# One fused two-block model on one Trainium2 core: conditioning groups reordered, their rows spread by the tensor engine, a thirteenth expert slot, the root table asked for ahead

## The reference, cut to what matters

```
def modulate(x, g, shift, scale):
    return rmsnorm(x, g) * (1 + scale) + shift

def ada_params(cvec, w, b):
    return jnp.split(jax.nn.silu(cvec) @ w + b, 6, axis=-1)
...
        sh1, sc1, g1, sh2, sc2, g2 = [a[:, None, :] for a in ada_params(c, ada_w[l], ada_b[l])]
        csh1, csc1, cg1, csh2, csc2, cg2 = ada_params(c_ctx, ada_w[l], ada_b[l])
        h_lat = modulate(x, norm_g[l, 0], sh1, sc1)
        h_ctx = modulate(ctx, norm_g[l, 0], csh1, csc1)
```

## Time and profile before

| | |
|---|---|
| median of 3 runs | 3414.62 us (3413.76 to 3415.18) |
| the profiled execution's own time | 3414.49 us |
| span of its trace | 3412.7 us |
| mean granted PE clock | 0.899 of full speed |
| busy: PE, DVE, ACT, POOL | 80%, 26%, 12%, 5% of the span |
| moved by DMA | 724.21 MB, mean 212 GB/s |

### The profile page before, as it was taken

The page is one execution under the profiler, slowest core; times in us unless marked ns, Lnnn a source line. Parts: engine busy times, 40 slices in busy tenths (PEclk is TensorE's granted clock), DMA queues, the critical chain, the costliest instruction groups (busy, mean ns, idle before and its releaser), DMA issues.

```text
span 3412.7 us, 31298 instructions
## 1 busy us (share of the span) xinstructions
PE 2740.5 (80%) x12274; PEld 1479.8 (43%) x12274; DVE 885.9 (26%) x1876; ACT 397.1 (12%) x760; POOL 174.2 (5%) x203
## 2 busy tenths in 40 slices
PE   5799876579979957689979987787794779877876
PEld 1344333334434424444457434443473754344433
DVE  1125624520020023420033311111354544111111
ACT  0113211110010010310000100000112111000001
POOL 1200000010010011010010100000000001000000
PEclk8899987789989978899989988988896989889888
DMA  8456469344434442044553599999640015899997
GB/s 267 123 172 207 137 226 291 117 142 148 147 127 141 152 136 68 1 167 147 197 170 114 225 392 396 405 393 390 244 148 0 5 76 190 345 393 404 392 391 300
DMA packets 318342, 724.21 MB, mean 212 GB/s; under 512 B 14111, under 2 KB 256175, under 8 KB 264367
## 3 DMA queue, kind: packets, MB, share of 16 engines
q1 hardware_dynamic: 306352, 690.01, 54.4%
q0 software_dynamic: 11904, 33.04, 2.8%
HBM read 721.79 MB, written 1.20 MB: 212 GB/s over the span
## 4 chain that ended last, share of the span: by engine, by line
PE 62%; DMA 21%; DVE 9%; SPq 3%; ACT 2%; issue 2%; POOL 1%; DVEq 0%; ACTq 0%; POOLq 0%
PE ps L807 24%; DMA ring<-in_moe_w_up 16%; PE ps L1324 9%; PE ps L912 6%; PE ps L832 5%; DMA ring<-in_ada_w 3%; PE ps L1012 3%; SPq L483 3%; PE ps L980 3%; PE ps L843 2%; PE ps L960 1%; PE ps L812 1%; PE ps L1265 1%; DVE h L1874 1%; DVE h L1872 1%
## 5 line engine op out<-in xcount | busy, mean ns | idle before, releaser
L807 PE MATMUL ps<-ring,hT 128*128 128x512 f32 x1856 | 826.0, 601 | 26.0 <-issue 8.1
L807 PEld LDWEIGHTS ps<-ring,hT 128*128 128x128 f32 x1856 | 354.5, 193 | 456.3 <-issue 443.3
L1324 PE MATMUL ps<-arena 128*32 128x512 f32 x1536 | 290.8, 731 | 118.8 <-DMA ring<-in_moe_w_up 115.8
L1324 PE MATMUL ps<-ring,arena 128*32 128x512 f32 x512 | 290.1, 732 | 0.0
L1314 PEld LDWEIGHTS ps<-arena,h 128*128 128x128 f32 x1024 | 248.5, 334 | 11.4 <-issue 7.7
L1314 PE MATMUL ps<-arena,h 128*128 128x128 f32 x1024 | 244.7, 398 | 0.0
L912 PE MATMUL ps<-ring,arena 128*128 128x512 f32 x528 | 232.2, 593 | 2.3 <-ACT arena L1552 2.3
L1324 PEld LDWEIGHTS ps<-arena 128*32 128x32 f32 x1536 | 68.5, 129 | 311.4 <-issue 189.9
L1920 DVE SCALAR_TENSOR_TENSOR arena<-ps,arena 128x256 f32<-128x256 f32 x66 | 28.0, 424 | 632.1 <-ACT arena L1548 632.1
L832 PE MATMUL ps<-hT,ring 128*128 128x256 f32 x768 | 169.8, 385 | 1.5 <-ACT hT L1482 1.5
L843 PE MATMUL ps<-ident,h 128*128 128x128 f32 x176 | 38.8, 392 | 152.9 <-DVE h L1874 152.9
(11 more groups left out here) (470 smaller groups left out, 2490.1 us busy)
## 6 DMA issues: line engine op xcount, KB each, us to landing
ring<-in_moe_w_down SPq DMA_DIRECT2D x128, 1024.0 KB, 19.0
ring<-in_ada_w SPq DMA_DIRECT2D x96, 1024.0 KB, 9.1
arena<-in_moe_w_gate SPq DMA_DIRECT2D x96, 1024.0 KB, 8.8
arena<-in_moe_w_up SPq DMA_DIRECT2D x96, 1024.0 KB, 10.9
ring<-in_ffn_w_in SPq DMA_DIRECT2D x66, 1024.0 KB, 8.5
ring<-in_ffn_w_out SPq DMA_DIRECT2D x33, 1024.0 KB, 5.1
ring<-in_moe_w_gate SPq DMA_DIRECT2D x32, 1024.0 KB, 16.4
ring<-in_moe_w_up SPq DMA_DIRECT2D x32, 1024.0 KB, 18.5
```

The lines of the kernel that those rows point to most:

```text
L807: m = pe.matmul(o3, lhsT_of(k), ring[:, a:a + 2, k * EH:(k + 1) * EH], start=start and k == 0, stop=stop and k == KC - 1)
L1324: m = pe.matmul(ps[a * CAP:(a + 1) * CAP, 6, :].rearrange("p (u c) -> p u c", u=2), x_slots[:, k, a * CAP:(a + 1) * CAP], slot_pair(GATE_U ...
```

## The change

It does five things.

- The start computes two groups (shift and scale of layer 0), not three, and by `ada_groups`. Their rows no longer go to memory and back: PE multiplies a column of `ident`, broadcast over 128 columns, with the rows and so spreads them to all partitions in PSUM (L1061 of the changed kernel); ACT copies the shifts, DVE makes the scales. All four token tiles are normed at once, and the `v` blocks stand between their transposes.
- The other 14 groups of the mixer's first half stand at places that `STEP_GROUPS` lists: one after `v`, `hg` and `gate`, then one or two in a scan step. The mLSTM has eight, one in each iteration. Group numbers now count from the start (0 to 23).
- Conditioning groups, `v`, `gate`, `qk`, `ml_v` and `ml_gate` load as double units: one transfer of 2 MB in 2 KB pieces into two neighbouring slots.
- A thirteenth slot of 1 MB takes turns with slot 6 for the first gate matrix of a quad, and that load is issued before the wait for `quad_gate_up_used`. `z_slots` moves into `x_sb`. The loop bodies of SP and PE hold two quads.
- `preload_act_table(ACT.Sqrt)` stands ahead of the wait in `update_tiles` and `update_and_norm`.

The diff, cut:

```diff
 
+    def two_slots(self):
+        self.pos += self.pos % 2
+        return self.slots(2)
...
-        ring_more = A(SLOTS, UNIT)
+        ring_more = A(SLOTS + 1, UNIT)
...
+        SPARE_SLOT = 2 * SLOTS
+        UP_SLOT = [7, 9, 11, 1]
+        GATE_SLOT = [[6, 8, 10, 0], [SPARE_SLOT, 8, 10, 0]]
         DOWN_SLOT = [2, 3, 4, 5]
...
-        ADA_B = (2, 1, 1, 1, 2, 1, 1, 1)
-        ADA_BEFORE_B = 3 + 8
+        ADA_B = (1,) * 8
+        FIRST_GROUPS = 2
...
+        STEP_GROUPS = ((5,), (6, 7), (8,), (9, 10), (11,), (12,), (13, 14), (15,))
...
+        SPREAD_BANK = [{1: 2, 0: 4}, {1: 6, 0: 0}]
...
+            def fill_two(s, src):
+
+                for each in (s, s + 1):
+                    if ada_free[each] > 0:
+                        sp.wait_ge(sem("ada_group_done"), ada_free[each])
+                        ada_free[each] = 0
+                    elif free_at[each] > 0:
+                        sp.wait_ge(block_done, free_at[each])
+                sp.dma_start(slot_two(s), src.rearrange("(p k) n -> p k n", k=KC)).then_inc(slot_filled[s], 16)
...
-                    for u, s in enumerate(n.slots(ADA_UNITS)):
-                        fill(s, kmajor(I[name][j][:, col + EH * u:col + EH * (u + 1)]))
-                        ada_free[s] = ada_next[0]
+                    for u in range(2):
+                        s, s1 = n.two_slots()
+                        fill_two(s, I[name][j][:, col + 2 * EH * u:col + 2 * EH * (u + 1)])
+                        ada_free[s] = ada_free[s1] = ada_next[0]
...
-                with sp.Fori(1, QUADS) as q:
-                    def expert(name, a):
-                        return I[name][l, bass.ds(q * QUAD + a, 1)].rearrange("o a b -> (o a) b")
-
-                    sp.wait_ge(used_gate_up, q + QUADS * l)
-                    for a in range(QUAD):
-                        gate_up_load(GATE_UP_SLOT[a], expert("moe_w_gate_2", a))
-                        gate_up_load(GATE_UP_SLOT[a] + 1, expert("moe_w_up_2", a))
-                    sp.wait_ge(used_down, q + QUADS * l)
+                def quad(expert, parity, done):
+
+                    gate_up_load(GATE_SLOT[parity][0], expert("moe_w_gate_2", 0))
+                    sp.wait_ge(used_gate_up, done)
+                    gate_up_load(UP_SLOT[0], expert("moe_w_up_2", 0))
+                    for a in range(1, QUAD):
+                        gate_up_load(GATE_SLOT[parity][a], expert("moe_w_gate_2", a))
+                        gate_up_load(UP_SLOT[a], expert("moe_w_up_2", a))
+                    sp.wait_ge(used_down, done)
                     for a in range(QUAD):
                         down_load(DOWN_SLOT[a], expert("moe_w_down_2", a))
+
+                with sp.Fori(0, QUADS // 2 - 1) as r:
+                    for j in range(2):
+                        quad(lambda name, a: I[name][l, bass.ds(r * (2 * QUAD) + ((1 + j) * QUAD + a), 1)].rearrange("o a b -> (o a) b"),
+                             1 - j, r * 2 + (1 + j + QUADS * l))
+                quad(lambda name, a: I[name][l, (QUADS - 1) * QUAD + a], 1, QUADS - 1 + QUADS * l)
                 n.block += 1
                 n.pos = 0
                 sp.wait_ge(used_gate_up, QUADS * (l + 1))
...
-            conditioning()
+            ada_groups(FIRST_GROUPS)
...
-            def two_units(at):
-                stream([kmajor(w[:, at + EH * j:at + EH * (j + 1)]) for j in range(2)], 4)
-
+            stream_two(w[:, 512:1024], 4)
+            ada_groups(1)
             for at in (0, 1536, 2048):
                 unit(at)
             ada_groups(1)
-            for at in (512, 1024):
-                two_units(at)
-                ada_groups(1)
-            for at in (0, 1536, 2048):
-                unit(at + EH)
-                ada_groups(1)
+            stream_two(w[:, 1024:1536], 4)
             ada_groups(1)
-            unit(2560)
+            unit(EH)
+            unit(1536 + EH)
+            ada_groups(3)
+            unit(2048 + EH)
+            ada_groups(3)
+            stream_two(w[:, 2560:3072], 4)
             ada_groups(1)
-            unit(2560 + EH)
-            two_units(3072)
-            ada_groups(2)
-            two_units(3584)
+            stream_two(w[:, 3072:3584], 4)
+            ada_groups(3)
+            stream_two(w[:, 3584:4096], 4)
             ada_groups(1)
...
+                    twos = [n.two_slots()[0] for _ in range(2)]
+                    for s in twos:
                         filled(s)
                     half = slice(EH * (g % 2), EH * (g % 2) + EH)
                     for k in range(KC):
-                        for u, s in enumerate(slots):
+                        for u in range(ADA_UNITS):
                             m = pe.matmul(ps[32 * u:32 * u + m_, bank, half], cond[:, lo:lo + m_, k],
-                                          ring[:, s, k * EH:(k + 1) * EH],
+                                          slot_two(twos[u // 2])[:, k, EH * (u % 2):EH * (u % 2 + 1)],
...
+            ada_groups(1, 1)
             pe.wait_ge(constants_loaded, 48)
-            norm_tiles(CTX)
-            norm_tiles(LAT)
-            pe.wait_ge(tp_evacuated, n.tp)
+            for g in range(2):
+                pe.wait_ge(sem("ada_rows_ready"), g + 1)
+                for r in (1, 0):
+                    for u in range(ADA_UNITS):
+                        one = ident[:, 32 * u + r:32 * u + r + 1].broadcast_to([P, P])
+                        m = pe.matmul(ps[:, SPREAD_BANK[g][r] + u // 2, EH * (u % 2):EH * (u % 2 + 1)], one, group_rows[:, g, :],
+                                      start=True, stop=True)
+                m.then_inc(sem("vectors_spread"), 1)
+            s = n.two_slots()[0]
+            for t in range(4):
+                b = n.h % 2
+                n.h += 1
+                pe.wait_ge(h_ready, n.h)
+                if t >= 2:
+                    pe.wait_ge(tp_evacuated, n.tp)
+                else:
+                    pe.wait_ge(sem("spread_read"), 2)
+                for half in range(2):
+                    transposes([h[:, b, 4 * half + kk::KC] for kk in range(4)])
+                pe.wait_ge(tp_evacuated, n.tp)
+                token_block(("v", t), s, t)
+            conditioning()
             for j in range(6):
-                unit_block(("hg", j), j % 2)
+                if j % 2 == 0:
+                    s = n.slots(1)[0]
+                unit_block(("hg", j), s, j % 2)
             conditioning()
+            s = n.two_slots()[0]
             for t in range(4):
-                token_block(("v", t), t)
...
+                    token_block(("ml_gate", 2), s_gate, 2)
+                    token_block(("ml_gate", 3), s_gate, 3)
+                for _ in STEP_GROUPS[i]:
+                    conditioning()
...
-                with pe.Fori(0, QUADS) as q:
-                    fg = lambda s: q * 16 + 16 + (16 * filled0[s] if s < SLOTS else more0)
-                    with pe.If(rounds > 1):
-                        with pe.Fori(1, rounds) as r:
-                            one_round(q * rounds + before + r - 1, fg)
-                    one_round(q * rounds + before + rounds - 1, fg, True)
+                with pe.Fori(0, QUADS // 2) as qq:
+                    for parity in range(2):
...
             def update_tiles(tiles, block_of):
 
+                nc.scalar.preload_act_table(ACT.Sqrt)
                 for i, t in enumerate(tiles):
...
-            norm_tiles(CTX)
-            norm_tiles(LAT)
+            act.wait_ge(sem("mean_square"), 1)
+            tell(nc.scalar.activation(stat[:, 1, 0:4], stat[:, 0, 0:4], ACT.Sqrt, scale=1.0 / D, bias=eps_t[:, :]), sem("rms_ready"))
+            act.wait_ge(sem("vectors_spread"), 1)
+            nc.scalar.copy(v_shift[:, :], spread_view(0, 1)).then_inc(sem("spread_read"), 1)
+            nc.scalar.copy(lat_shift, spread_view(0, 0)).then_inc(sem("spread_read"), 1)
+            n.normed = 1
...
+            for t in range(4):
+                do(V.tensor_tensor_reduce(out=h[:, 0, :], in0=x_sb[:, t, :], in1=x_sb[:, t, :], scale=1.0,
+                                          scalar=0.0, op0=ALU.mult, op1=ALU.add, accum_out=stat[:, 0, t:t + 1]))
+            tell(V.tensor_copy(note[:, :], eps_t[0:1, :]), sem("mean_square"))
+            dve.wait_ge(sem("rms_ready"), 1)
+            do(V.reciprocal(stat[:, 2, 0:4], stat[:, 1, 0:4]))
+            n.normed = 1
+            ada_rows(1, 0)
+            ada_rows(1, 1)
+            dve.wait_ge(sem("vectors_spread"), 2)
+            dve.wait_ge(sem("vectors_loaded"), 16)
+            for r, dst in ((1, v_scale[:, :]), (0, lat_scale)):
+                do(V.scalar_tensor_tensor(out=dst, in0=spread_view(1, r), scalar=1.0, in1=v_tmp[:, :], op0=ALU.add, op1=ALU.mult))
+            dve.wait_ge(sem("spread_read"), 2)
+            for t in range(4):
+                b = n.h % 2
+                if h_turned[b]:
+                    dve.wait_ge(tp_full, h_turned[b])
```

(52 more changed lines are left out.)

230 lines of the change are left out of this document (111 added, 119 removed).

## The result

The changed kernel takes 3364.4 us (median of 4 runs, 3357.1 to 3365.9) against 3414.9 of the kernel before on the same chip: ratio 0.9848, interval [0.9833, 0.9864]. The forecast was 3324 us, 3303 to 3346. The direction held; the gain is 51 us where 91 were forecast.

A forecast was written before the change was run, and what follows sets the result against it. PE held 62% of the chain and DMA 21%; the first mixer, expert loops and sublayer ends mattered. 3414.5 - 18 (mixer) - 65 (experts) - 7.7 (root table) = 3324 us, range 3303 to 3346.

The forecast's parts named there:

- The price of a double: Loads of 2 MB in 2 KB pieces: 5.4 us each at 388 GB/s, 8.45 from a freed pair, 13.85 for two.
- Front: First mixer until the scan starts: start at 181 us instead of 229.85, gain 49 us.
- Scan: First mixer's scan: waits for loads in steps 1, 3, 5 and 6 make it 309 us instead of 241.9, 67 lost.
- mLSTM: End of the first mixer: eight groups instead of ten, period 13.75 us instead of 14.3, over at 602, gain 36.
- Second rival: Mixer: doubles run at 348 GB/s, so it gains 4 us, not 18; 3338 us; chance 17%.
- Experts: Both expert layers: DMA's hole is filled, periods of 29.75 us, 65 us gained (40 if holes of 0.9 stay).
- third rival: Experts: hole only half filled, PE at its lower clock arrives last; 32 us instead of 65, 3357 us; chance 11%.
- Fourth rival: Expert loops: bodies of two quads make each turn fetch code; 63 us more in 30 periods, 3451 us; chance 4%.
- Root table: Norms: six table loads of 1283 ns behind a Square get hidden by waits for the sums; 7.7 us gained, bounds 4 to 7.7.

The follow-up runs named there:

- ksplit: Changed kernel with every double unit as two transfers of 1 MB that keep the 2 KB pieces (cut by rows); 3343.2 us, ratio 0.9783.
- slots: Changed kernel with two slots skipped ahead of groups 6 and 13 and ahead of `ml_v`, order on PE unchanged; 3325.0 us, ratio 0.9737.
- units: Changed kernel with every double unit split into two transfers of 1 MB in 1 KB pieces; 3354.7 us, ratio 0.9822.
- experts_only: Kernel before with only the thirteenth slot, the early gate load and the loop bodies of two quads; 3361.8 us, ratio 0.9844.
- no_preload: Changed kernel without the two early requests for the root table; 3371.9 us, ratio 0.9880.
- halves: Changed kernel with a group's two doubles cut by rows (4 KB pieces) instead of by columns; 3311.0 us, ratio 0.9691.

## Why the prediction was off, step by step

- **The price of a double is the step that failed:** "5.4 us a double (6.03 to 4.93), 8.45 us from a freed pair, 13.85 for two". It measured 9.5 us on the mean for one (9.3 to 10.5 in the mLSTM) and 15.7 to 15.8 for two. The larger part is what came on top of the rate. It was taken from a lone 1 MB unit, 3.05 us, and kept for a transfer twice as long; at the 368 GB/s that the mLSTM's landings show on the mean, the bytes take 5.7 us and 3.8 are left, an estimate. The smaller part is the rate, 352 to 380 GB/s against 388. The bounds of the term held only the rate, and so were too narrow. It goes into the waits ahead of five groups of the scan, the front and eight periods. With ksplit, where each transfer is again 1 MB, both come back to the forecast: 377 to 399 GB/s, 8.5 us on the mean to PE's start, a scan of 309.7 us (forecast 309), and 22 us for the kernel. Of the 24.5 us that the mixer fell short (-18 forecast, +6.5 in the trace), 16 come back in its own profiled mixer (627.7 to 612.0 beside the changed kernel).
- **Front:** +49 forecast, 45.7 measured (229.85 to 184.15). The step that failed is the time at which group 0's slots are free: it landed at 23.3 and was done at 29.4 us, where the forecast had them free at 24, and the double of group 1 came 9.4 us later, so that group 1 started at 38.8, not 32.6. Why group 0 landed so late was not tried. From there to the first `v` block it took 20.2 us as forecast (20.4); half of the delay was made up by shorter `v` blocks and `hg` blocks.
- **Scan:** the place of each wait was right, and slots shows the mechanism for the three that it removes. 309 us forecast, 316.5 measured; the five waits ahead of groups are 6.8 us over their price.
- **mLSTM:** 15.36 is 13.75, 1.1 for the double, 0.4 for the group and 0.1 for the issue. In every second iteration the group took 6.3 to 6.4 us, not 5.3. The forecast took 4.9 to 5.8 for a group behind a wait, but the trace of the kernel before also has two of 6.4 in the mLSTM (at 496.53 and 554.50). The mean granted clock of this stretch is 0.77 (510 to 626 us).
- **Second rival (3338 us, doubles at 348 GB/s):** its time for the mixer (a gain of 4, measured a loss of 6.5) was nearer than mine, and so was its price, 9.1 us for one double and 15.1 for two. Its rate was nearly right for doubles as one transfer (352 to 380 GB/s), but the size of the pieces was not the reason, since the same pieces reach 377 to 399 in ksplit. "DMA: Bandwidth & Descriptors" of the Trainium skill, section Specifications, has line rate from 512 B on; by that rule ksplit and units, with pieces of 2 and 1 KB, would be equal, and they differ by 13 us. The measurement decides against it here.
- **Experts:** 65 forecast, 54 alone and 55.8 in the trace. The place and the hole were right. Two sizes were off. The full rate is 420 to 422 GB/s in windows of 24 us without a dip, not the 425 of one window before, which makes 29.9 us a quad instead of 29.6. And dips stay behind the slow products: 14 of the 28 quads have a window of 1 us under 380 GB/s. The third rival (PE the last to arrive) was seen, nearly without its price.
- **Fourth rival:** the page has 62 code transfers of 1.02 MB (57 of 0.93 before), five more for the 30 quads that the loops go on with, so a turn of a loop does not fetch code.
- **Root table:** 7.7 us was right alone (7.9). In the changed kernel only 2.2 us are left outside mixer and experts: from the mixer's end to quad 0 it takes 1312.6 us (1312.3 before), between the layers 491.9 (491.3), after the last quad 30.7 (33.6). The six loads behind a Square are gone; nine early ones stand in their place, one in each call. Where some of the time was lost again can be seen: there are stretches in which PE ran at a lower clock than in the same code before, in the attention and behind it for instance; of the changed kernel:

```profile
1392.00:1400.00 8.00, 7.09 (x28) 4.79 (x28) 2.67 (x7) 2.21 (x6) 0.00 (x0) 0.68 0.00 1
...
1445.98 9.94 PE L835 MATMUL ps<-ring,hT 128*128 128x512 f32 x16 [3.03 <-DVE hT L2368]
```

and of before:

```profile
1386.70:1394.00 7.30, 6.27 (x28) 4.45 (x28) 2.79 (x7) 2.32 (x6) 0.00 (x0) 0.80 0.00 0
...
1439.84 8.83 PE L807 MATMUL ps<-ring,hT 128*128 128x512 f32 x16 [3.03 <-DVE hT L2293]
```

Why the clock rose later in these places was not tried, and whether it makes up the whole is not shown. The stretch from mixer to quad 0 takes 1315.6 us in experts_only, whose code there is that of before: 3.3 us more, with no edit in it. It takes 1317.0 in no_preload and 1309.1 to 1312.9 in the profiled runs of the changed kernel, its repetition, units, ksplit, slots and halves. So the trace of the kernel before, with 1312.3, is short for a kernel without the early loads, and a sum of small gains can't be read from one pair of traces to better than 3 us.

## What to carry to other kernels

Price a load that something waits for as issue to landing, from a row of a transfer of the same size; two transfers of 1 MB in 2 KB pieces landed 0.9 us sooner than one of 2 MB with the same bytes, and which is better is decided only where a wait hangs on it. Before making loads cheaper, follow each to its slot and ask who reads the slot last: skipping six slots gave 40 us, and cutting a group by rows, so that its first half is used and given back early and its pieces are larger, gave 55, more than the whole change. And do not put two users of the same slots side by side if other work can stand between them.
